# One column by transposes, fewer running-sum products, later operands 128 bytes further on, and one DVE order changed

## The chip, the cores and the metric

The kernel is one program on one core of a Trainium2 chip. The metric is the device time of one execution in microseconds (us); smaller is better. The engines are named as the profile names them: PE is TensorE's matmuls, PEld its loads of the stationary operand, DVE is VectorE, ACT is ScalarE, POOL is GpSimd, SP is the engine that issues most DMAs.

## The reference

The input is 256 tokens of width 1024, all in float32. A first block computes `h @ w_in` and splits it into four branches (a gated delta rule in chunks of 64, latent attention, spatial gating, forgetting attention), gates and sums them, and follows with `w_out` and a squared-ReLU feed-forward of width 4096. A second block has two layers: a state-space mixer with a short convolution, then sliding-window attention, each with a SwiGLU feed-forward of width 2816 and a gated embedding. What the change touches is four pieces of it:

```
# gated delta rule                              # chunks of 64 tokens
gc = jnp.cumsum(g, axis=-1)
decay = jnp.where(tril, jnp.exp(gc[..., :, None] - gc[..., None, :]), 0.0)
kb = k * beta[..., None]
# forgetting attention
cum = jnp.cumsum(log_f, axis=1)
s = s + (cum[..., :, None] - cum[..., None, :])
# state-space mixer                             # chunks of 128 tokens, 16 heads
a_cs = jnp.cumsum(da, axis=2)
decay_ls = jnp.exp(jnp.where(causal, a_cs[t] - a_cs[s], -jnp.inf))
y_diag = jnp.einsum('bclsgr,bcsgrp->bclgrp', cb[..., None] * decay_ls, xdt)
y = (y_diag + y_off + xs * d_skip) * jax.nn.silu(z)
```

Each of these decays needs a running sum over tokens twice: down the partitions (a column, one value for each token) and along a row that all partitions hold.

## The kernel before, in words

**Products.** Nearly all work is products of 256 tokens with weight matrices. Weights stream in units of 1024 columns: SP brings a unit into `raw`, ACT copies it to `whi` in the format fp32r (the high half), POOL subtracts and leaves the low half in `wlo`, and PE multiplies. Every product is made of three passes: high by high, high by low, low by high (function `product`, L1942 on; `unit_T`, L1910 on, is the same with one token tile at a time; `half`, L2145 on, is half a unit). In mode T the tokens' operand is stationary and 512 columns of `whi` or `wlo` move (L1960 to L1962, L1918 to L1920, L2167 to L2169); in modes F and B the weights are stationary and the tokens in `XT` move.

**Where the operands lie.** `raw`, `whi`, `wlo`, `X` and `XT` are allocated first; `whi`, `wlo` and `XT` start 128 bytes past a multiple of 256 in each partition. The split operands of the other stages (`BRhi`, `FFhi`, `PThi`, `BYhi`, `Hhi`, `AThi` and their low halves) are allocated later and start at a multiple of 1024 (`MQhi`, `MQlo`: 192 past a multiple of 256). All steps within these buffers are multiples of 512 bytes.

**Order of the work.** Each engine's order is written out by hand, with semaphores between the engines. PE's order interleaves the chained small work (the `mm` calls, all recorded as L1982, and transposes) with units of products, which fill PE's time while DVE and ACT work.

**Running sums and rows.** A running sum down the partitions is a small `mm` with a triangle of ones as stationary operand. A row was made by `mm` with the un-summed column, spread over 128 columns, as stationary operand and the triangle as moving one; for `beta`, with the identity.

**State-space heads.** There are eight groups of four heads (`hb` = 0 to 7). For a group, PE makes four rows (`rows`), DVE subtracts the column and masks (`decays`, L1627), ACT takes the exponential, DVE multiplies by the scores (`products`, L1636), and PE multiplies by the values (`heads_out`). After each second group DVE adds the other parts and gates the pair's output (`finished`, L1643 and L1647). `heads_out` of the next pair writes the same bank of PSUM and waits for that (`b_yd`); it also waits for its own `products` (`b_m`). PE's fill between the groups is half units of the products `sc0` and `sh0`.

Of the kernel before, what the change touches and what calls it, by code (L numbers as in the profile page):

```python
# [22 lines left out]
P = 128  # L23
# [202 lines left out]
def build(nc, a, out):  # L226
# [8 lines left out]
    with ctx:  # L235
# [55 lines left out]
        attn_sum = attn_sum2[:, 0]  # L291
        attn_inv2 = sb("attn_inv2", [P, 2, 4, 2])
        attn_inv = attn_inv2[:, 0]


        m1 = ExitStack()
# [782 lines left out]
        def _(v):  # L1079
# [551 lines left out]
            def products(hb):  # L1631
                v.wait_ge(S["b_e"], hb + 1)
                if hb >= 4:

                    v.wait_ge(S["b_y"], hb - 3)
                V.scalar_tensor_tensor(out=em[:, hb % 4], in0=pm[:, row_bank(hb), :].rearrange("p (r s) -> p r s", s=P),  # L1636
                                       scalar=1.0, in1=cbm[:, hb // 2, :].unsqueeze(1).to_broadcast([P, 4, P]),
                                       op0=ALU.min, op1=ALU.mult).then_inc(S["b_m"], 1)

            def finished(b):  # L1640
                y = yd[:, b // 2, (b % 2) * W:(b % 2 + 1) * W]
                v.wait_ge(S["b_y"], 2 * b + 2)
                link(V.tensor_tensor(pm[:, 2, :], pm[:, 2, :], y, ALU.add))  # L1643
                v.wait_ge(*evac_at("dt"))
                for c in range(2):
                    v.wait_ge(*evac_at(f"mz{c}"))
                V.tensor_tensor(y, pm[:, 2, :], zz[:, b // 2, (b % 2) * W:(b % 2 + 1) * W], ALU.mult)\  # L1647
                    .then_inc(S["b_yd"], 1)
            decays(0)
            decays(1)  # L1650
            for hb in range(8):
                products(hb)
                if hb < 6:
                    decays(hb + 2)
                if hb % 2:
                    finished(hb // 2)
            short_input(0)
            v.wait_ge(S["y_ss"], 1)
            link(variance(rv[:, 0:4], ss[:, 0:4], W, 1e-5))
# [207 lines left out]
        def _(pe):  # L1867
# [113 lines left out]
            def mm(o, lhs, rhs, start=True, stop=True, **k):  # L1981
                return T.matmul(o, lhs, rhs, start=start, stop=stop, **k)  # L1982

            def flat(i, n=P):

                return pm[:, i // BANK, i % BANK:i % BANK + n]


            def keep_busy(count):

# [38 lines left out]

            pe.wait_ge(S["dn_qkn"], 1)  # L2030
            pe.wait_ge(S["dn_g"], 1)
            for t in range(NT):
                mm(pm[:, 0, 4 * t:4 * t + 4], con("tri64"), dng[:, t, :])
                mm(pm[:, 0, 8 + 4 * t:12 + 4 * t], con("blk64"), dng[:, t, :])
            mm(pm[:, 0, 16:20], con("tri"), nlf[:, 0, :])
            mm(pm[:, 0, 20:24], ones, nlf[:, 0, :], stop=False)
            mm(pm[:, 0, 20:24], con("tri"), nlf[:, 1, :], start=False).then_inc(S["dn_gc"], 1)
            from_x("fq", 0, 2)
            pe.wait_ge(S["dn_gcs"], 1)

            for h in range(4):
                for t in range(NT):
                    i = (h * NT + t) * P
                    mm(flat(i), dng[:, t, h:h + 1].to_broadcast([P, P]), con("tri64"))
                    last = mm(flat(2 * BANK + i), beta[:, t, h:h + 1].to_broadcast([P, P]), ident)
            last.then_inc(S["dn_rows"], 1)
            from_x("fq", 2, 4)
            from_x("fk", 0, 1)
# [179 lines left out]
            pe.wait_ge(*turned("cqkv")(1))  # L2228
            for h in range(4):
                row = pm[:, 2 + h // 2, (h % 2) * TOK:(h % 2 + 1) * TOK]  # L2230
                mm(row, nlf[:, 0, h:h + 1].to_broadcast([P, P]), span("tri", "ones"), stop=False)
                last = mm(row[:, P:TOK], nlf[:, 1, h:h + 1].to_broadcast([P, P]), con("tri"), start=False)
            last.then_inc(S["f_rows"], 1)
            from_branch("br0_1")
            product("uq0", MQhi[:, 0:2], MQlo[:, 0:2])
# [111 lines left out]
            for g in range(2):  # L2347
                last = T.transpose(pm[:, 3, g * P:(g + 1) * P], xbcT[:, 8 + g, 0:P], ident)
            last.then_inc(S["s_bt"], 1)
            for c in range(2):  # L2350
                mm(pm[:, 3, 2 * P + c * SSD_H:2 * P + (c + 1) * SSD_H], con("tri"), da[:, c, :])
            mm(pm[:, 3, 2 * P + 2 * SSD_H:2 * P + 3 * SSD_H], ones, da[:, 0, :]).then_inc(S["s_ac"], 1)
            from_x("mz1", 1, 3)
            pe.wait_ge(S["s_btc"], 1)
# [10 lines left out]
            def rows(hb):  # L2365

                c, first = hb // 4, 8 * (hb // 2 % 2) + 4 * (hb % 2)
                if hb >= 3:
                    pe.wait_ge(S["b_m"], hb - 2)
                elif hb == 2:  # L2370
                    pe.wait_ge(S["s_yod"], 1)
                for r in range(4):
                    last = mm(pm[:, row_bank(hb), r * P:(r + 1) * P],
                              da[:, c, first + r:first + r + 1].to_broadcast([P, P]), con("tri"))
                last.then_inc(S["b_row"], 1)

            def heads_out(hb):

                b, half = hb // 2, hb % 2
                pe.wait_ge(S["b_m"], hb + 1)  # L2380
                if b and not half:
                    pe.wait_ge(S["b_yd"], b)
                for r in range(4):
                    at = (4 * half + r) * SSD_D
                    x = (b % 2) * W + at
                    last = mm(pm[:, 2, at:at + SSD_D], em[:, hb % 4, r, :], xdt[:, b // 2, x:x + SSD_D])
                last.then_inc(S["b_y"], 1)
            rows(0)
            rows(1)
            from_x("sc0", 0, 1)  # L2390
# [229 lines left out]
```

## Time and profile before

| | |
|---|---|
| time, median of 3 runs | 1267.34 us (1266.71 to 1269.21) |
| the profiled execution's own time | 1270.26 us |
| its span, first to last instruction | 1268.4 us |
| mean granted clock of TensorE | 0.997 |
| PE busy | 1258.0 us, 99% of the span, 7611 instructions |
| DVE, ACT, POOL busy | 39%, 51%, 74% |
| DMA | 218.33 MB, mean 172 GB/s |

A float32 matmul (`mm`) leaves two records of PE; an fp32r product or a transpose leaves one. A record's duration holds the way through the array and overlaps the next one, so that what a matmul costs is read as the distance from its start to the next start.

### The profile page before, as it was taken

What the parts mean: (1) busy time and instruction counts of PE and PEld (TensorE: products, weight loads), DVE (VectorE), ACT (ScalarE), POOL (GpSimd) and SP (SyncE); (2) the same over time, 40 slices, a digit from 0 to 9 for tenths busy, and PEclk for the clock granted to TensorE, in tenths of its full rate; (3) what the DMA queues carried; (4) which work ended last, traced back from release to release, by engine and by line L of the source; (5) the groups of instructions that cost most, each with busy time, mean ns of one, the idle gap of its engine ahead of it and who ended that gap; (6) DMA issues with size and microseconds to landing.
All of it is one profiled execution on the core that took longest, in us unless ns stands there. A gap on an engine that the chain in (4) does not pass through costs nothing.

```text
span 1268.4 us, 18665 instructions
## 1 busy us (share of the span) xinstructions
PE 1258.0 (99%) x7611; PEld 1081.4 (85%) x7611; DVE 490.5 (39%) x893; ACT 650.3 (51%) x873; POOL 942.5 (74%) x409
## 2 busy tenths in 40 slices
PE   9999999999999999999999999999999999999998
PEld 7988888888888888899999788888879868888886
DVE  5535344552224320037662153332042674333025
ACT  5573555755457653344544464444355655444433
POOL 6946357756969898875588688889867666888964
PEclk9999999999999999999999999999999999999999
DMA  8735235534646655553456566665548435655641
GB/s 285 211 116 165 70 100 164 183 101 139 224 142 208 194 202 194 190 166 112 150 167 199 196 227 190 192 199 184 198 125 277 152 119 161 185 183 183 202 163 67
DMA packets 147739, 218.33 MB, mean 172 GB/s; under 512 B 9368, under 2 KB 79559, under 8 KB 147655
## 3 DMA queue, kind: packets, MB, share of 16 engines
q1 hardware_dynamic: 143664, 209.73, 52.2%
q10 hardware_dynamic: 3990, 7.42, 1.8%
q8 instruction: 60, 0.98, 0.3%
q14 instruction: 25, 0.20, 0.0%
HBM read 216.07 MB, written 1.05 MB: 171 GB/s over the span
## 4 chain that ended last, share of the span: by engine, by line
PE 96%; DVE 2%; DMA 1%; ACT 0%; POOL 0%; issue 0%; POOLq 0%; ACTq 0%; DVEq 0%
PE acc L1966 18%; PE acc L1960 13%; PE acc L1961 12%; PE acc L1962 12%; PE acc L1967 9%; PE pm L1982 7%; PE acc L1973 4%; PE acc L1975 4%; PE acc L1976 4%; PE acc L1918 2%; PE acc L1920 1%; PE acc L1919 1%; PE acc L2167 1%; PE acc L2169 1%; PE acc L2168 1%; PE pm L1880 1%
## 5 line engine op out<-in xcount | busy, mean ns | idle before, releaser
L581 POOL TENSOR_TENSOR wlo<-raw,whi 128x1024 fp32r<-128x1024 f32 (+4 forms) x404 | 941.8, 2358 | 313.9 <-ACT whi L595 312.8
L595 ACT ACTIVATE whi<-raw 128x1024 fp32r<-128x1024 f32 (+4 forms) x404 | 404.6, 1033 | 225.3 <-PE acc L1962 143.0
L1966 PE MATMUL acc<-XT,whi 128*128 128x512 f32 x960 | 335.6, 395 | 0.0
L1967 PE MATMUL acc<-XT,wlo 128*128 128x256 f32 x960 | 268.1, 279 | 0.0
L1966 PEld LDWEIGHTS acc<-XT,whi 128*128 128x128 f32 x960 | 180.0, 188 | 42.2
L1967 PEld LDWEIGHTS acc<-XT,wlo 128*128 128x128 f32 x960 | 181.0, 189 | 0.0
L1973 PE MATMUL acc<-XT,whi 128*128 128x256 f32 x432 | 123.2, 285 | 0.0
L1960 PE MATMUL acc<-whi,XT 128*128 128x512 f32 (+4 forms) x320 | 123.0, 385 | 0.0
L1976 PE MATMUL acc<-XT,wlo 128*128 128x256 f32 x432 | 122.2, 283 | 0.0
L1975 PE MATMUL acc<-XT,whi 128*128 128x256 f32 x432 | 122.2, 283 | 0.0
L1961 PE MATMUL acc<-wlo,XT 128*128 128x512 f32 (+4 forms) x320 | 119.5, 373 | 0.0
L1962 PE MATMUL acc<-whi,XT 128*128 128x512 f32 (+4 forms) x320 | 119.5, 373 | 0.0
L1973 PEld LDWEIGHTS acc<-XT,whi 128*128 128x128 f32 x432 | 82.9, 192 | 0.6 <-issue 0.5
L1975 PEld LDWEIGHTS acc<-XT,whi 128*128 128x128 f32 x432 | 82.9, 192 | 0.1
L1976 PEld LDWEIGHTS acc<-XT,wlo 128*128 128x128 f32 x432 | 82.8, 192 | 0.0
L1960 PEld LDWEIGHTS acc<-whi,XT 128*128 128x128 f32 x320 | 60.1, 188 | 11.6 <-issue 1.5
L1962 PEld LDWEIGHTS acc<-whi,XT 128*128 128x128 f32 x320 | 60.2, 188 | 10.1
L1961 PEld LDWEIGHTS acc<-wlo,XT 128*128 128x128 f32 x320 | 60.2, 188 | 9.4 <-issue 0.5
L595 ACT ACTIVATE Hhi<-pm 128x512 fp32r<-128x512 f32 x22 | 13.2, 598 | 83.9 <-DVE pm L1769 83.9
L1961 PE MATMUL acc<-wlo,Hhi 128*128 128x512 f32 x136 | 53.7, 395 | 0.0
L1960 PE MATMUL acc<-whi,Hhi 128*128 128x512 f32 x136 | 53.7, 395 | 0.0
L1962 PE MATMUL acc<-whi,Hlo 128*128 128x512 f32 x136 | 53.6, 394 | 0.0
(413 smaller groups left out, 1986.2 us busy)
## 6 DMA issues: line engine op xcount, KB each, us to landing
raw<-in_w_in SPq DMA_DIRECT2D x68, 512.0 KB, 3.5
raw<-in_w_ff SPq DMA_DIRECT2D x64, 512.0 KB, 3.8
raw<-in_w_gate SPq DMA_DIRECT2D x44, 512.0 KB, 3.6
raw<-in_w_up SPq DMA_DIRECT2D x44, 512.0 KB, 3.6
raw<-in_w_down SPq DMA_DIRECT2D x44, 512.0 KB, 4.0
raw<-in_w_in_mix SPq DMA_DIRECT2D x36, 512.0 KB, 4.1
raw<-in_w_branch SPq DMA_DIRECT2D x16, 512.0 KB, 3.7
raw<-in_w_out_mix SPq DMA_DIRECT2D x16, 512.0 KB, 3.2
```

The source lines that it names most:

```text
L581: nc.gpsimd.tensor_tensor(piece(wlo, u), piece(raw, u), piece(whi, u).bitcast(F32), ALU.subtract).then_inc(S["w_lo"], 1)
L595: return nc.scalar.activation(out_, in_, func, **k)
L1918: T.matmul(o, hi[:, k, tok], wh, start=k == 0 and name not in CONTINUED, stop=False)
L1960: T.matmul(o, hi[:, k, tok], wh, start=opens, stop=False)
L1961: T.matmul(o, hi[:, k, tok], wl, start=False, stop=False)
L1962: last = T.matmul(o, lo[:, k, tok], wh, start=False, stop=done)
L1966: T.matmul(acc[:, n % 2, f, :], wh[:, fs], XT[:, :, k, :], start=opens, stop=False)
L1967: last = T.matmul(acc[:, n % 2, f, 0:TOK], wl[:, fs], XThi[:, k, :], start=False, stop=done)
L1973: T.matmul(o, wh[:, fs], hi[:, k, :], start=opens and f % 2 == 0, stop=False, skip_group_check=True)
L1975: T.matmul(o, wh[:, fs], lo[:, k, :], start=False, stop=False, skip_group_check=True)
L1976: last = T.matmul(o, wl[:, fs], hi[:, k, :], start=False, stop=done, skip_group_check=True)
L1982: return T.matmul(o, lhs, rhs, start=start, stop=stop, **k)
```

## The change

There are four edits. A buffer `apart` of 128 bytes, which nothing uses, is allocated before all later buffers, so that these start 128 bytes further on. The rows are made by PE transposes of a column: of the summed column (`gcs`, `ncs`, `acs`) that DVE has already written, or of `beta`, spread over 128 columns as before. Running sums of the same triangle are put into one `mm` each. On DVE `finished` of a pair is placed behind the `products` of the next group. Before the first rows of the state-space heads PE also waits for `s_acc`, the summed columns.

```diff
+        sb("apart", [P, 32])
...
             decays(0)
             decays(1)
-            for hb in range(8):
+            products(0)
+            decays(2)
+            for hb in range(1, 8):
                 products(hb)
+                if hb % 2 == 0:
+                    finished(hb // 2 - 1)
                 if hb < 6:
                     decays(hb + 2)
-                if hb % 2:
-                    finished(hb // 2)
+            finished(3)
...
+            def row_of(o, col):
+
+                return T.transpose(o, col.to_broadcast([P, P]), ident)
...
-            for t in range(NT):
-                mm(pm[:, 0, 4 * t:4 * t + 4], con("tri64"), dng[:, t, :])
-                mm(pm[:, 0, 8 + 4 * t:12 + 4 * t], con("blk64"), dng[:, t, :])
-            mm(pm[:, 0, 16:20], con("tri"), nlf[:, 0, :])
-            mm(pm[:, 0, 20:24], ones, nlf[:, 0, :], stop=False)
-            mm(pm[:, 0, 20:24], con("tri"), nlf[:, 1, :], start=False).then_inc(S["dn_gc"], 1)
+            both = [ap.rearrange("p t h -> p (t h)") for ap in (dng[:], nlf[:])]
+            mm(pm[:, 0, 0:8], con("tri64"), both[0])
+            mm(pm[:, 0, 8:16], con("blk64"), both[0])
+            mm(pm[:, 0, 16:24], con("tri"), both[1])
+            mm(pm[:, 0, 20:24], ones, nlf[:, 0, :], start=False, skip_group_check=True).then_inc(S["dn_gc"], 1)
...
-                    mm(flat(i), dng[:, t, h:h + 1].to_broadcast([P, P]), con("tri64"))
-                    last = mm(flat(2 * BANK + i), beta[:, t, h:h + 1].to_broadcast([P, P]), ident)
+                    row_of(flat(i), gcs[:, t, h:h + 1])
+                    last = row_of(flat(2 * BANK + i), beta[:, t, h:h + 1])
...
-                mm(row, nlf[:, 0, h:h + 1].to_broadcast([P, P]), span("tri", "ones"), stop=False)
-                last = mm(row[:, P:TOK], nlf[:, 1, h:h + 1].to_broadcast([P, P]), con("tri"), start=False)
+                for t in range(NT):
+                    last = row_of(row[:, t * P:(t + 1) * P], ncs[:, t, h:h + 1])
...
-            for c in range(2):
-                mm(pm[:, 3, 2 * P + c * SSD_H:2 * P + (c + 1) * SSD_H], con("tri"), da[:, c, :])
+            mm(pm[:, 3, 2 * P:2 * P + 2 * SSD_H], con("tri"), da[:].rearrange("p c h -> p (c h)"))
...
-                    last = mm(pm[:, row_bank(hb), r * P:(r + 1) * P],
-                              da[:, c, first + r:first + r + 1].to_broadcast([P, P]), con("tri"))
+                    last = row_of(pm[:, row_bank(hb), r * P:(r + 1) * P], acs[:, c, first + r:first + r + 1])
...
+            pe.wait_ge(S["s_acc"], 1)
             rows(0)
             rows(1)
```

How the instructions stand on DVE in the state-space heads before: `pm<-pm,acs,ct` is `decays` (x4, x8: four for each group), `em<-pm,cbm` is `products`, and the pair of `TENSOR_TENSOR` rows is `finished`.

```order
L1627 SCALAR_TENSOR_TENSOR pm<-pm,acs,ct 128x128 x8
L1636 SCALAR_TENSOR_TENSOR em<-pm,cbm 128x512
L1627 SCALAR_TENSOR_TENSOR pm<-pm,acs,ct 128x128 x4
L1636 SCALAR_TENSOR_TENSOR em<-pm,cbm 128x512
L1627 SCALAR_TENSOR_TENSOR pm<-pm,acs,ct 128x128 x4
L1643 TENSOR_TENSOR pm<-pm,yd 128x512
L1647 TENSOR_TENSOR yd<-pm,zz 128x512
L1636 SCALAR_TENSOR_TENSOR em<-pm,cbm 128x512
L1627 SCALAR_TENSOR_TENSOR pm<-pm,acs,ct 128x128 x4
```

And the same place of DVE now, one line number up:

```order
L1628 SCALAR_TENSOR_TENSOR pm<-pm,acs,ct 128x128 x8
L1637 SCALAR_TENSOR_TENSOR em<-pm,cbm 128x512
L1628 SCALAR_TENSOR_TENSOR pm<-pm,acs,ct 128x128 x4
L1637 SCALAR_TENSOR_TENSOR em<-pm,cbm 128x512
L1628 SCALAR_TENSOR_TENSOR pm<-pm,acs,ct 128x128 x4
L1637 SCALAR_TENSOR_TENSOR em<-pm,cbm 128x512
L1644 TENSOR_TENSOR pm<-pm,yd 128x512
L1648 TENSOR_TENSOR yd<-pm,zz 128x512
L1628 SCALAR_TENSOR_TENSOR pm<-pm,acs,ct 128x128 x4
```

The third `products` stands ahead of the first `finished` where it stood behind it, and so for each pair.

On PE, before, around the third group's rows (`pm<-ct,da`) and the first `heads_out` (`pm<-xdt,em`):

```order
L1975 MATMUL acc<-XT,whi 128x256
L1976 MATMUL acc<-XT,wlo 128x256
L1982 MATMUL pm<-ct,da 128x128 x4
L1982 MATMUL pm<-xdt,em 128x64 x4
L1982 MATMUL pm<-ct,da 128x128 x4
L2158 MATMUL acc<-XT,whi 128x256
```

And now (L1994 is the transpose in `row_of`):

```order
L1979 MATMUL acc<-XT,whi 128x256
L1980 MATMUL acc<-XT,wlo 128x256
L1994 MATMUL pm<-ct,acs 128x128 x4
L1986 MATMUL pm<-xdt,em 128x64 x4
L1994 MATMUL pm<-ct,acs 128x128 x4
L2164 MATMUL acc<-XT,whi 128x256
```

Nothing has changed its place on PE; the four matmuls of a group of rows are four transposes of `acs`. ACT, POOL and SP have the same rows in the same order before and now.

## Rows read from the trace of the kernel before

**Rows 1.** The page: the chain that ended last, share of the span by engine.

```profile
PE 96%; DVE 2%; DMA 1%; ACT 0%; POOL 0%; issue 0%; POOLq 0%; ACTq 0%; DVEq 0%
```

**Rows 2.** Waits of all engines: who waited for whom.

```profile
POOL wlo L581 <- ACT whi L595: 312.8, 159, 10.7
```

**Rows 3.** Timeline of PE, stationary operand `XT`: start us, duration us.

```profile
309.87 0.39 PE L1961 MATMUL acc<-wlo,XT 128*128 128x512 f32 x1
...
331.18 0.40 PE L1962 MATMUL acc<-whi,XT 128*128 128x512 f32 x1
```

**Rows 4.** Timeline of PE, stationary operand `FFhi` or `FFlo`.

```profile
484.92 0.39 PE L1961 MATMUL acc<-wlo,FFhi 128*128 128x512 f32 x1
...
508.38 0.40 PE L1960 MATMUL acc<-whi,FFhi 128*128 128x512 f32 x1
508.63 0.40 PE L1961 MATMUL acc<-wlo,FFhi 128*128 128x512 f32 x1
```

**Rows 5.** Groups by line and shape: count, busy us, mean ns, idle before.

```profile
L1961 PE MATMUL acc<-wlo,XT 128*128 128x512 f32 x240 | 93.6, 390 | 0.0
L1961 PE MATMUL acc<-wlo,Hhi 128*128 128x512 f32 x136 | 53.7, 395 | 0.0
```

**Rows 6.** Timeline of PE: the running sums of the first block.

```profile
75.19 0.95 PE L1982 MATMUL pm<-dng,ct 128*128 128x4 f32 x8
...
76.67 0.48 PE L1960 MATMUL acc<-whi,XT 128*128 128x512 f32 x1
```

**Rows 7.** Timeline of PE: the delta rule's rows, first one and what follows them.

```profile
82.21 0.38 PE L1982 MATMUL pm<-ct,dng 128*128 128x128 f32 x2
...
85.70 0.48 PE L1960 MATMUL acc<-whi,XT 128*128 128x512 f32 x1
```

**Rows 8.** Timeline of PE: the forgetting attention's rows.

```profile
206.59 2.78 PE L1982 MATMUL pm<-ct,nlf 128*128 128x256 f32 x16
209.13 0.47 PE L1960 MATMUL acc<-whi,BRhi 128*128 128x512 f32 x1
```

**Rows 9.** Timeline of PE: sixteen transposes.

```profile
252.98 1.91 PE L2260 MATMUL pm<-ct,fx 128*128 128x128 f32 x16
254.65 0.48 PE L1960 MATMUL acc<-whi,BRhi 128*128 128x512 f32 x1
```

**Rows 10.** Timeline of PE: state-space heads.

```profile
618.68 1.00 PE L1982 MATMUL pm<-xdt,em 128*128 128x64 f32 x8
619.52 1.11 PE L1982 MATMUL pm<-ct,da 128*128 128x128 f32 x8
620.39 0.36 PE L2158 MATMUL acc<-XT,whi 128*128 128x256 f32 x1
...
621.91 1.00 PE L1982 MATMUL pm<-xdt,em 128*128 128x64 f32 x8
...
625.12 1.00 PE L1982 MATMUL pm<-xdt,em 128*128 128x64 f32 x8
```

**Rows 11.** Timeline of DVE, same stretch.

```profile
617.81 0.68 DVE L1636 SCALAR_TENSOR_TENSOR em<-pm,cbm 128x512 f32<-128x512 f32 x1
...
622.94 0.70 DVE L1643 TENSOR_TENSOR pm<-pm,yd 128x512 f32<-128x512 f32 x1 [1.14 <-PE pm L1982]
623.68 0.69 DVE L1647 TENSOR_TENSOR yd<-pm,zz 128x512 f32<-128x512 f32 x1
```

**Rows 12.** Timeline of ACT, same stretch.

```profile
622.85 1.07 ACT L595 ACTIVATE pm<-pm 128x512 f32<-128x512 f32 x2
```

**Rows 13.** Timeline of PE: the longest wait.

```profile
1043.48 1.12 PE L1890 MATMUL pm<-ct,X 128*128 128x128 f32 x4 [2.61 <-DVE X L1695]
```

**Rows 14.** Stretches: length, busy (count) by engine, granted clock, DMA share, GB/s.

```profile
1046.00:1050.00 4.00, 4.00 (x11) 3.14 (x10) 3.75 (x10) 2.49 (x5) 1.18 (x1) 0.50 0.79 253
...
613.00:642.00 29.00, 29.00 (x251) 28.86 (x250) 20.17 (x49) 14.82 (x22) 12.87 (x7) 1.00 0.33 105
243.00:255.00 12.00, 12.00 (x79) 10.55 (x78) 1.78 (x2) 6.64 (x6) 8.73 (x4) 1.00 0.60 189
```

## The prediction

> **What bounds the kernel.** I read the chain of waits first. 96% of the span is PE's own work [rows 1], so a us less of PE's work is a us less of time wherever PE doesn't then wait for another engine. The waits say how much room the others have: POOL waits 312.8 us in all for ACT's high halves [rows 2] while its share of the span is 74%, and ACT is at 51%, so the weights keep up with a PE that is 1% faster. PE's one long wait is 2.61 us at 1043 us, on DVE's layer norm [rows 13]; no edit shortens it. So I price each edit on PE, from start to start in its timeline, and then look at the one place where DVE and ACT are nearly as late as PE: the state-space heads [rows 10 to 12].
>
> **Price of a transpose.** A row of 128 columns is now a float32 matmul of two records. The delta rule has 16 of them between 82.21 and 85.70 us: 3.49 / 16 = 0.218 us each [rows 7]. Sixteen transposes take 252.98 to 254.65: 1.67 / 16 = 0.104 us each [rows 9]. I read starts, since the mean durations of the two kinds are about equal and would show no gain. The trace has no transpose of a column spread over 128 columns. Its bounds are these two prices, 0.104 and 0.218 us. I take the lower, because spreading costs an ordinary matmul nothing: the `heads_out` matmuls, whose stationary operand isn't spread, take 618.68 to 619.52, 0.84 / 4 = 0.21 us each [rows 10], as much as the spread ones.
>
> **Delta rule.** The rows save 16 x (0.218 - 0.104) = 1.8 us. What waits for them on DVE and ACT starts from their end, and PE's fill behind them is unchanged, so nothing is late that wasn't. The running sums are seven small matmuls in 75.19 to 76.67, 1.48 us or 0.21 each [rows 6]; four remain. A matmul of eight columns instead of four is still bound by its weights at this size, so three go: 0.6 us.
>
> **Forgetting attention.** Eight matmuls take 206.59 to 209.13, 2.54 us [rows 8]; eight transposes take 8 x 0.104 = 0.8. Saved: 1.7 us. No engine is near waiting for these rows, since DVE works on the gating until then. The state-space running sum loses one small matmul: 0.2 us.
>
> **State-space heads.** 32 matmuls become transposes. In full this would be 32 x 0.114 = 3.6 us, but here little of it arrives. I follow PE with the old times. Three groups of rows stand ahead of the first `heads_out`, so PE is ready for it 3 x 0.45 = 1.3 us before 618.68. DVE's first `products` runs 617.81 to 618.49 [rows 11], and what stands ahead of it on DVE is the gating of the state's output, which starts when it did. `heads_out` starts at 618.6: 0.1 us gained, 1.2 us of a wait. Then 0.84 of `heads_out`, 0.42 of rows, and 1.52 of fill (620.39 to 621.91), the same again, and PE is ready for the third `heads_out` at 624.2, 0.9 before the old 625.12 [rows 10].
>
> There the moved instruction decides. Before, `finished` ran when the second `heads_out` was done, at 622.94, and the third `products` behind it. Now `products` goes first, and it needs the exponential that ACT makes at 622.85, behind a table load and the gate's activation; two take 1.07 us, so the first is there at 623.4 [rows 12]. ACT doesn't get there sooner, since its work from the first exponential on is unbroken. `products` ends at 624.1 (0.68 us), `finished` at 625.5 (0.70 + 0.69 and the gap between them), and PE starts the third `heads_out` at 625.6, 0.5 us later than before and 1.4 us after it was ready. Behind `products` stand `finished` and the fifth group's `decays` on DVE; who waits for them is PE alone. In the later pairs the exponential is early, so from 625.6 on the groups of rows still to come pass their gain on: three behind that point, 3 x 0.45 = 1.3. In sum the stage gives 1.3 - 0.5 = 0.8 us. In the old DVE order `finished` would be done at 623.9 and the third `heads_out` would start at about 624.6; so the new order costs 0.7 to 1 us here. Bounds of the stage: from 0.5 us lost (nothing passes behind the wait) to 3.6 gained. I take 0.8. The added wait for `s_acc` costs nothing: DVE writes these sums before PE's last two units of `mz1`, which stand ahead of the rows in PE's order.
>
> **The 128 bytes.** Two stretches of the same three-pass product differ only in where the stationary operand lies. With `XT`, 94 matmuls take 309.87 to 331.18: 21.31 / 94 = 226.7 ns each [rows 3]. With `FFhi` and `FFlo`, 102 take 484.92 to 508.63: 23.71 / 102 = 232.5 ns [rows 4]. The grouped view says it for all: mean duration 390 ns with `XT`, 395 with `Hhi` [rows 5]. `XT` has the same offset modulo 256 bytes as the moving `whi` and `wlo` (128), the others have 0; after the change all have 128. The matmuls with such an operand are, by the code, (16 + 32 + 16 + 44 + 8 + 4) k tiles of branches, f2, mo, fd, ao and pw x 2 column halves x 2 token tiles x 3 passes = 1440. If the offset is the cause, each gets 5 ns (the grouped means; 5.8 by the two stretches): 1440 x 5 = 7.2 us. The trace can't tell offset from place, since `XT` is also the only one of these operands allocated early. Bounds: 0, and 1440 x 5.8 = 8.4; the other side is rival B. I take the 7.2: the two stretches share everything but this operand, moving slots and banks of PSUM included.
>
> **Sum.** 1.8 + 0.6 + 1.7 + 0.2 + 0.8 + 7.2 = 12.3 us. Against the profiled execution: 1270.26 - 12.3 = 1258.0, with a span of 1256.1. That execution stands 2.9 above the median, which makes 1267.34 - 12.3 = 1255.0; I say 1255.2.
>
> **Rivals.**
> A, the offset does nothing. For it: the pace could hang on the place, and no row excludes this. Against it: `FFhi` and `Hhi` begin 28 KB apart and share the slower pace [rows 4, 5], as they share the offset. The time: only 5.1 us go, 1262.2. The Trainium skill, TensorE: Matmul & The Clock Gate, Step-by-step: what each phase is for, says that moving and stationary operands have read ports of their own, so that loading the next weights takes no bandwidth from the running matmul. By that rule addresses play no part and A holds; the 226.7 against 232.5 ns speak against it, or want another cause.
>
> B, slower: equal offsets make the two reads meet. The place is the same 1440 matmuls. Slow steps exist in the trace: 508.38 to 508.63 is 0.25 us between two starts [rows 4]. If the pace became 241 ns, 1440 x 8.6 = 12.4 us would be added and 5.1 saved: 1274.6. It decides from a pace of 236 ns on (1440 x 3.5 = 5.1). Against it: `XT` has this very offset and is the fast one.
>
> C, the spread column as a transpose is as dear as the matmul. Then rows give nothing: 0.8 us of running sums, 7.2, and in the heads a loss of 0.5 by the order: 1267.3 - 7.5 = 1259.8. Nothing but the missing row speaks for it.
>
> D, the new waits slow the clock. Behind the 2.61 us wait [rows 13] the granted clock is 0.50 from 1046 to 1050 [rows 14], level 1.2 GHz in place of 2.4. The two waits that I expect in the heads, 1.2 and 1.4 us, are shorter and 7 us apart, and now that stretch has 1.00. If it fell for as long, 4 to 6 us at half pace would cost 2 to 3 us: 1258. The Trainium skill, same page, Part 4: PE-mode transpose, says that transposes don't count as busy for the clock. By that rule the 56 new ones would add to the risk; 48 transposes between 243 and 255 us leave the clock at 1.00 [rows 14], so I raise D by a few hundredths only.
>
> **Chances.** The forecast (all terms, 1252.5 to 1258) 0.56; A 0.28; B 0.04; C 0.04; D 0.05; the rest, 0.03, is something unseen. A range from 1252.5 to 1263.3 holds the forecast, A with 1 us around it, C and D. What a measurement of this kernel can tell from no change is 0.2%, 2.5 us: faster means below 1264.8. Forecast, A, C and D all are; allowing for errors of sizes in A, faster 0.89, within 0.2% 0.06, slower 0.05 (B).
>
> **What would show it.** The `row_of` records start 0.104 to 0.11 us apart, one for each row. PE's 1440 matmuls run at 227 to 228 ns from start to start, mean duration 390; at 232 A is right, above 236 B. In the heads PE waits twice, before the first `heads_out` (1.2 us, for `products`) and before the third (1.4, for `finished`), and the third `products` on DVE starts right after ACT's exponential, ahead of the first `finished`. The stretch from the first rows to the last `heads_out` is only 0.8 us shorter. The forecast is wrong if PE's busy matmuls don't change their pace, or if PE waits anywhere else for DVE or ACT.

## The result, and the profile after

Runs of the two kernels taken by turns on one chip:

| | median | range | runs |
|---|---|---|---|
| before | 1269.19 us | 1266.71 to 1270.38 | 7 |
| after | 1263.77 us | 1258.29 to 1264.14 | 7 |

The ratio is 0.995 (95% interval 0.9938 to 0.9962): faster by 5.4 us of the medians, where 12.3 were forecast. The time lies 8.6 us above the forecast 1255.2 and above its range; 1.9 of the 8.6 are the kernel before itself, whose median is now 1269.19 and not the 1267.34 that the forecast started from. The profiled execution of after took 1263.77 us, its span 1261.9, 6.5 less than the span before.

The chain of waits of after, by engine; it answers to [rows 1]:

```profile
PE 91%; DVE 4%; ACT 2%; DMA 1%; issue 1%; POOL 1%; ACTq 0%; POOLq 0%; DVEq 0%
```

PE still carries it, but DVE and ACT have risen from 2% to 6% together: there are waits that weren't there. The waits of PE in after name most of them (line waited for: us in total, times, longest):

```profile
PE pm L1894 <- DVE X L1699: 3.9, 4, 2.7
PE acc L1964 <- DVE merged L1386: 1.5, 1, 1.5
PE pm L1986 <- DVE yd L1648: 1.4, 1, 1.4
...
PE pm L1986 <- DVE em L1637: 1.1, 1, 1.1
```

The first is the layer norm's wait of [rows 13]. `yd` and `em` are the two waits in the state-space heads that the prediction gave 1.4 and 1.2 us. `merged` is new and wasn't forecast. Two smaller ones are new as well, from PE's timeline in after:

```profile
603.81 1.96 PE L1986 MATMUL pm<-xe,bmt 128*128 128x512 f32 x4 [0.27 <-DVE xe L1584]
...
984.76 0.88 PE L2475 MATMUL pm<-ct,wS 128*128 128x128 f32 x6 [0.48 <-DVE wS L1841]
```

The own operands' matmuls (stationary `FFhi`, `Hhi` and so on) by start, in after; they answer to [rows 4]:

```profile
483.27 0.39 PE L1965 MATMUL acc<-wlo,FFhi 128*128 128x512 f32 x1
...
506.39 0.39 PE L1965 MATMUL acc<-wlo,FFhi 128*128 128x512 f32 x1
```

102 matmuls in 23.12 us are 226.7 ns each, the pace that only `XT` had [rows 3]. The grouped means of after answer to [rows 5] and bring a third row into play, the 960 products in which `XT` moves and `whi` is stationary (L1966 before, L1970 now):

```profile
L1970 PE MATMUL acc<-XT,whi 128*128 128x512 f32 x960 | 339.6, 399 | 0.0
L1965 PE MATMUL acc<-wlo,XT 128*128 128x512 f32 x240 | 93.6, 390 | 0.0
L1965 PE MATMUL acc<-wlo,Hhi 128*128 128x512 f32 x136 | 52.9, 389 | 0.0
```

In the trace of before, which the prediction didn't read there, the same group is:

```profile
L1966 PE MATMUL acc<-XT,whi 128*128 128x512 f32 x960 | 335.6, 395 | 0.0
```

`Hhi` went from 395 to 389 ns as forecast and `XT` as stationary operand stayed at 390, while the 960 went from 395 to 399. That is a loss inside busy time: no view of waits can show it.

Where the span's 6.5 us came from, start to start on PE in the two traces:

| part | forecast | profile pair |
|---|---|---|
| own operands' pace | -7.2 | -7.6 |
| delta rule's rows | -1.8 | -1.8 |
| running sums, block 1 and state space | -0.8 | -0.8 on PE, +0.2 as a wait for `xe` |
| forgetting rows | -1.7 | -1.7 on PE, +1.7 as a wait |
| heads | -0.8 | -0.9 |
| `XT` products with `XT` moving | not priced | +4.0 |
| a wait for the embedding's `wS` at 984 us | not priced | +0.7 |
| sum | -12.3 | -6.2 (span: -6.5) |

**The forgetting rows.** PE in after, behind the spatial gating's sums; it answers to [rows 8]:

```profile
203.99 1.04 PE L1994 MATMUL pm<-ct,ncs 128*128 128x128 f32 x8
204.79 0.48 PE L1964 MATMUL acc<-whi,BRhi 128*128 128x512 f32 x1
...
212.05 0.45 PE L1964 MATMUL acc<-whi,MQhi 128*128 128x384 f32 x1 [1.54 <-DVE merged L1386]
```

and DVE in the same stretch:

```profile
204.19 1.67 DVE L1393 SCALAR_TENSOR_TENSOR pm<-pm,colA,s_b 128x256 f32<-128x256 f32 x4 [6.16 <-PE pm L1986]
205.90 1.23 DVE L1398 TENSOR_TENSOR pm<-pm,sgu 128x1024 f32<-128x1024 f32 x1
207.04 0.34 DVE L1402 SCALAR_TENSOR_TENSOR fD<-pm,ncs,ct 128x128 f32<-128x128 f32 x1
...
209.65 1.22 DVE L1408 TENSOR_TENSOR BRlo<-pm,BRhi 128x1024 fp32r<-128x1024 f32 x1
210.78 2.35 DVE L1386 TENSOR_TENSOR merged<-acc,gt 128x1024 f32<-128x1024 f32 x2
```

The rows take 0.80 us (203.99 to 204.79), as forecast. But DVE's chain starts when PE's `swT` sums end, just ahead of the rows: gating, eight `fD` decays, `BRlo`, and only then `merge(0, 0)` (L1386), which empties the accumulator that the first `MQhi` product needs. The chain is as long as before. PE's stretch between the sums and that product is now 1.7 us shorter and starts to wait: the step onto `MQhi` is 1.93 us instead of 0.23.

**The moving `XT` products.** In these stages (f1 of block 1 with 256 pairs, the SwiGLU products of both layers with 352 each) a 512-column matmul with `whi` and a 256-column one with `wlo` alternate. In after:

```profile
779.80 0.40 PE L1970 MATMUL acc<-XT,whi 128*128 128x512 f32 x1
...
790.40 0.40 PE L1970 MATMUL acc<-XT,whi 128*128 128x512 f32 x1
```

30 pairs in 10.60 us are 353.3 ns a pair. In another execution of the same kernel (`e7_after_again` below), at the same place:

```profile
779.57 0.39 PE L1970 MATMUL acc<-XT,whi 128*128 128x512 f32 x1
...
789.97 0.39 PE L1970 MATMUL acc<-XT,whi 128*128 128x512 f32 x1
```

10.40 us for 30, 346.7 ns. From start to start there are two repeating patterns: 230, 117 ns over and over (in some stretches 231, 112, 233, 117, which is as long for a pair), or 241, 120, 236, 113, 233, 117. A stretch takes one of them in its first few matmuls and keeps it to its end. In f1 this happens behind a short break: its first eight pairs run in the slow sequence in every profile of this order, and the pattern is taken anew behind the small matmuls that follow them. The slow one (S) costs 1.7 us in f1 and 2.4 in each layer's stage over the fast one (F). Before's profile has F, F, S for the three stretches, after's S, S, S: 1.7 + 2.4 = 4.1 us, the table's 4.0. The means of the group of 960 tell it without any timeline: 392 ns where all three stretches are fast, 395 with one layer slow, 399 with all slow.

### The profile page after: what moved, and what is told of

Read it like the earlier page. It is cut to its first block, busy times and chain, and to the rows that moved or that the text cites. A ratio compares the mean times of both kernels' runs of the same rounds, so it can differ in the third digit from the quotient of the medians.

```text
span 1261.9 us, 18537 instructions
## 1 busy us (share of the span) xinstructions
PE 1246.5 (99%) x7547; PEld 1072.8 (85%) x7547; DVE 490.8 (39%) x893; ACT 650.1 (52%) x873; POOL 941.6 (75%) x409
## 4 chain that ended last, share of the span: by engine, by line
PE 91%; DVE 4%; ACT 2%; DMA 1%; issue 1%; POOL 1%; ACTq 0%; POOLq 0%; DVEq 0%
PE acc L1970 18%; PE acc L1964 12%; PE acc L1965 12%; PE acc L1966 12%; PE acc L1971 9%; PE pm L1986 6%; PE acc L1977 4%; PE acc L1979 4%; PE acc L1980 4%; PE acc L1922 2%; PE acc L1923 1%; PE acc L1924 1%; PE acc L2173 1%; PE acc L1999 1%; PE acc L2175 1%; PE acc L2174 1%
## 5 line engine op out<-in xcount | busy, mean ns | idle before, releaser
L1970 PE MATMUL acc<-XT,whi 128*128 128x512 f32 x960 | 339.6, 399 | 0.0
L1970 PEld LDWEIGHTS acc<-XT,whi 128*128 128x128 f32 x960 | 180.4, 188 | 44.9
L1966 PE MATMUL acc<-whi,XT 128*128 128x512 f32 (+4 forms) x320 | 119.4, 373 | 0.0
L1966 PEld LDWEIGHTS acc<-whi,XT 128*128 128x128 f32 x320 | 60.1, 188 | 10.0
L1966 PE MATMUL acc<-whi,Hlo 128*128 128x512 f32 x136 | 52.9, 389 | 0.0
```

The source lines that it names most:

```text
L1966: last = T.matmul(o, lo[:, k, tok], wh, start=False, stop=done)
L1970: T.matmul(acc[:, n % 2, f, :], wh[:, fs], XT[:, :, k, :], start=opens, stop=False)
```

## The experiments

All medians are in us, with their range; the ratios are to before on the same chip. F and S are the patterns of the three stretches in the profiled execution. The heads are the stretch from the first rows to the start of the matmul behind the last `heads_out`. The medians of before beside these runs were 1269.70 (e1 to e4), 1269.37 (e5 to e8), 1269.38 (e9 to e12) and 1269.15 (e13, e14).

| run | edit | median (range) | ratio, 95% interval | pattern | heads |
|---|---|---|---|---|---|
| e1 | before, `apart` 128 bytes | 1264.02 (1262.72 to 1266.65) | 0.9955, 0.9942 to 0.9968 | F S S | 28.55 |
| e2 | after, no `apart` | 1265.44 (1264.61 to 1266.80) | 0.9968, 0.9956 to 0.9980 | F F S | 27.60 |
| e3 | after, DVE's old order | 1259.45 (1258.24 to 1261.87) | 0.9923, 0.9911 to 0.9935 | S S F | 27.01 |
| e4 | before, `apart` 256 bytes | 1269.80 (1266.65 to 1274.32) | 1.0000, 0.9990 to 1.0011 | F F S | 28.54 |
| e5 | e3, merge early | 1261.19 (1256.09 to 1263.49) | 0.9933, 0.9916 to 0.9950 | F S S | 27.00 |
| e6 | after, merge and rows early | 1256.06 (1255.06 to 1257.58) | 0.9895, 0.9880 to 0.9911 | S S F | other start |
| e7 | after again, one execution | 1258.82 | | S F F | 27.61 |
| e8 | before again, one execution | 1267.08 | | F F F | 28.53 |
| e9 | e6, merge earlier still | 1255.80 (1255.08 to 1258.36) | 0.9890, 0.9876 to 0.9904 | F S F | other start |
| e10 | e9, grouped pairs | 1254.14 (1253.53 to 1254.44) | 0.9873, 0.9860 to 0.9885 | steady | other start |
| e11 | after, unwaited entry | 1262.92 (1259.52 to 1264.12) | 0.9938, 0.9922 to 0.9955 | S S F | |
| e12 | after, old forgetting rows | 1262.61 (1259.67 to 1263.95) | 0.9936, 0.9921 to 0.9950 | S S S | |
| e13 | before, grouped pairs | 1268.71 (1268.34 to 1269.50) | 1.0001, 0.9992 to 1.0011 | steady | 28.54 |
| e14 | after, grouped pairs | 1258.71 (1258.35 to 1260.22) | 0.9924, 0.9910 to 0.9939 | steady | 27.61 |

**e1 and e2: the 128 bytes alone, and all the rest alone.** e1 is before with one line more, e2 is after without it:

```
+        sb("apart", [P, 32])
```

> The kernel before with the 128 bytes alone. Theory P (offset sets the pace): the 1440 matmuls with FF, H, BY, BR, AT, PT operands run at 227 ns from start to start, 7.5 to 8 us less. Theory L (the shift also drives the products with XT moving in two pieces, L1966 and L1967, into their slow repeating pattern of 353.4 ns a pair instead of 346.7): all three stretches with such products (f1, the first and the second fg/fu) are at 353.4, and the net is 8 minus 4 = 4 us faster than the profiled before. Rival C (that pattern falls by chance, whatever the layout): the three stretches show a mixture of 346.7 and 353.4, and single executions of one kernel differ in steps of 1.7 and 2.4 us (256 and 352 pairs x 6.7 ns).

> The changed kernel without the 128 bytes: transposes, joined sums and the new DVE order alone. Theory P: the 1440 matmuls are back at 232.4 ns. PE saves 1.8 + 0.6 + 0.2 us, 0.9 in the heads, and the forgetting rows' 1.7 are eaten by a wait of 1.7 before uq0, so 3.3 to 3.5 us faster than before at the same pattern of the XT products. Theory L: the XT products are at 346.7 ns a pair in f1 and the first fg/fu as in the profile of before. Rival C: a mixture that differs from before's.

In e1 the own operands' matmuls run at 227.1 ns instead of 232.4, all other steps as before; the time falls by about 5.7 us, not 7.6, with two slow stretches in its profile. In e2 they run at 232.4, and it is 4.3 us below before by the medians and 3.5 by the two profiled executions, which both have F F S (3.3 to 3.5 were expected), with the `merged` wait and the heads as in after. So the pace belongs to the shift and nothing else, and the `merged` wait doesn't.

**e4: the same line with 256 bytes.** It moves every later buffer too, but leaves the offset modulo 256.

```
+        sb("apart", [P, 64])
```

> The kernel before with 256 bytes in place of 128: the later operands move, but their offset modulo 256 is as before. Theory P (the offset against whi and wlo): pace stays at 232.4 ns, time as before. Rival A (place, not offset, or the new neighbours): pace changes, to 227 if any move does it.

The own pace stays at 232.6 and the time at 1269.8. The grouped rows, first e1 (128 bytes), then e4 (256); with `XT` the mean is 390 ns in both:

```profile
L1967 PE MATMUL acc<-XT,whi 128*128 128x512 f32 x960 | 338.0, 397 | 0.0
L1962 PE MATMUL acc<-wlo,Hhi 128*128 128x512 f32 x136 | 52.9, 389 | 0.0
```

```profile
L1962 PE MATMUL acc<-wlo,Hhi 128*128 128x512 f32 x136 | 53.7, 395 | 0.0
```

It is the offset modulo 256 bytes that counts, not the place: what the trace of before couldn't tell is told. The moving `whi` and `wlo` stay 128 past a multiple of 256 in every run, so it isn't shown whether the distance between the two operands sets the pace or the stationary one's own offset. The Trainium skill, TensorE: Matmul & The Clock Gate, Step-by-step: what each phase is for, has it that loading weights takes no read bandwidth from the running matmul. Read as rival A read it, as a rule in which addresses play no part, it doesn't fit the 232.4 against 227.2 ns; the measurement decides.

**e3: DVE's old order in the heads.**

```
-            products(0)
-            decays(2)
-            for hb in range(1, 8):
+            for hb in range(8):
...
-                if hb % 2 == 0:
-                    finished(hb // 2 - 1)
...
-            finished(3)
+                if hb % 2:
+                    finished(hb // 2)
```

> The changed kernel with the DVE order of before in the heads. Theory O (the new order costs here): PE's wait before the third heads_out falls from 1.57 to about 0.4 us, the first stays at 1.2, a third small one of 0.3 may come before the fifth, and the stage from the first rows to the last heads_out is 0.7 us shorter than the changed kernel's 27.6. Rival N (the order is neutral or helps): the stage is as long or longer.

The heads take 27.01 us against 27.61. DVE in e3, around the third `products`:

```profile
618.79 0.70 DVE L1644 TENSOR_TENSOR pm<-pm,yd 128x512 f32<-128x512 f32 x1 [1.15 <-PE pm L1983]
619.52 0.69 DVE L1648 TENSOR_TENSOR yd<-pm,zz 128x512 f32<-128x512 f32 x1
620.13 0.68 DVE L1637 SCALAR_TENSOR_TENSOR em<-pm,cbm 128x512 f32<-128x512 f32 x1
```

against the same in after:

```profile
619.53 0.69 DVE L1637 SCALAR_TENSOR_TENSOR em<-pm,cbm 128x512 f32<-128x512 f32 x1 [2.20 <-ACT pm L596]
620.14 0.69 DVE L1644 TENSOR_TENSOR pm<-pm,yd 128x512 f32<-128x512 f32 x1
```

In the new order DVE waits 2.20 us for ACT's exponential with `finished` behind it; in the old one `finished` fills that time. The new order costs 0.6 us; the prediction said 0.7 to 1. The median fell by 4 us, far more than this 0.6. That is what first pointed at something that no edit had touched, and e3's profile has a fast third stretch.

**e5, e6 and e9: taking the waits away.** e5 is e3 with `merge(0, 0)` ahead of the `fD` decays:

```
     (spatial gating)
+            merge(0, 0)
     (decays of the forgetting attention, BRlo)
-            merge(0, 0)
```

> The changed kernel with the old DVE order in the heads (as the run before it with that order) and DVE's first gating product, merge(0, 0), ahead of the forgetting attention's decays instead of behind them. Theory M (the forgetting rows were the cover of DVE's chain to merge(0, 0), which frees the accumulator for uq0): PE's wait of 1.7 us before the first MQ matmul goes, and the time is 1.5 to 1.7 us below that run at the same patterns of the XT products. Rival (the wait has another end, such as the weights of uq0): it stays.

DVE in e5:

```profile
206.31 1.23 DVE L1398 TENSOR_TENSOR pm<-pm,sgu 128x1024 f32<-128x1024 f32 x1
207.45 1.21 DVE L1386 TENSOR_TENSOR merged<-acc,gt 128x1024 f32<-128x1024 f32 x1
208.58 0.34 DVE L1403 SCALAR_TENSOR_TENSOR fD<-pm,ncs,ct 128x128 f32<-128x128 f32 x1
```

and PE, at the starts of the two products with this operand (`uq0`, `uq1`):

```profile
210.75 0.34 PE L1961 MATMUL acc<-whi,MQhi 128*128 128x384 f32 x1
...
213.58 0.45 PE L1961 MATMUL acc<-whi,MQhi 128*128 128x384 f32 x1 [0.58 <-DVE merged L1386]
```

The first `MQhi` product no longer waits (a step of 0.23 us in place of 1.93): `merge(0, 0)` was what PE waited for. But `merge(0, 1)`, which stands behind the decays and `BRlo` as before, is now late for the second one, onto which the step is 0.92 us. So 1.7 us go and 0.7 come back 2.8 us later. (What was expected of e9 takes these 0.92 us for a rest of the first wait.) The median didn't follow (1261.19, with a range of 7.4 us): the profile has two slow stretches. A gain of 1 us can't be read from medians that scatter so; it is read in the trace.

e6 has the new DVE order and the early merge, and in the heads two groups ahead of the wait for the state: `rows(0)` and `rows(1)` on PE before the state-output product, their decays on DVE before its gating:

```
+            pe.wait_ge(S["s_acc"], 1)
+            rows(0)
+            rows(1)
             pe.wait_ge(S["s_stc"], 1)
     (state-output product)
...
     (DVE: decays(0), decays(1), and then)
+            v.wait_ge(S["s_yo"], 1)
+            V.tensor_tensor(by_head(off), by_head(off), per_head(eac[:, 0, :]), ALU.mult)
```

> The changed kernel (new DVE order kept) with merge(0, 0) ahead as in the run beside it, and in the heads rows(0), rows(1) and their decays ahead of the state's output product and its gating. Theory H (PE's two waits of 1.2 and 1.6 us come from DVE's gating standing ahead of the first decays, and from ACT's second exponential pair behind a table load): both waits fall below 0.3 us, the stage from the first product of the state's output to the last heads_out is 2.3 to 2.7 us shorter, and the new order is the better one here. Rival: the waits only move, to the state's output product or to heads_out of the second pair.

Both waits of the heads are gone. From the first of rows and state-output product to the matmul behind the last `heads_out` it is 26.5 us in e6 against 29.3 in after, 2.8 less; 2.3 to 2.7 were expected. The first three `heads_out` in e9, which shares this part, come without one; from the second to the third it is 2.71 us, against 4.27 in after (617.43 to 621.70):

```profile
610.09 1.10 PE L1986 MATMUL pm<-xdt,em 128*128 128x64 f32 x8
...
612.89 1.00 PE L1986 MATMUL pm<-xdt,em 128*128 128x64 f32 x8
...
615.60 1.00 PE L1986 MATMUL pm<-xdt,em 128*128 128x64 f32 x8
```

e9 is e6 with `merge(0, 0)` still earlier, ahead of DVE's wait for the spatial sums, where it was idle 4 us and more:

> The kernel of e6 (rows early, new DVE order) with merge(0, 0) still earlier on DVE: ahead of the spatial gating's sums. Theory M: the rest of PE's wait before the first MQ matmul (0.92 us from start to start in e6, where an unwaited step is 0.23) goes, so 0.7 us less than e6 at the same patterns of the XT products. Rival: DVE's later start on the gating makes BRlo of branch 2 or the decays late, and PE waits there instead.

```profile
202.56 1.22 DVE L1386 TENSOR_TENSOR merged<-acc,gt 128x1024 f32<-128x1024 f32 x1 [4.41 <-PE acc L1966]
204.35 1.67 DVE L1394 SCALAR_TENSOR_TENSOR pm<-pm,colA,s_b 128x256 f32<-128x256 f32 x4 [0.56 <-PE pm L1986]
```

The merge costs nothing there, `merge(0, 1)` is done earlier too, and PE waits before neither of the two `MQhi` products. The medians of e6 and e9 are equal within their scatter.

**e7 and e8: the same two kernels once more.**

> The changed kernel once more. Theory C (the pattern of the XT products is latched when each of the three stretches is entered, by chance of a few ns): at least one of the three stretches may be at 346.8 ns a pair instead of 353.5, and span and stretches agree: 1.7 us for f1, 2.4 for each fg/fu stretch. Theory L (the shift fixes it): all three at 353.5 again.

> The kernel before once more. Theory C: the three stretches may differ from 347, 347, 353.5 ns a pair. Theory L: they are the same again.

These two executions settle what the 4.0 us are. Nothing was edited, and after came at 1258.82 with S F F, 4.9 us below its first profile with S S S (2 x 2.4 = 4.8); before at 1267.08 with F F F, 3.2 below its first with F F S (2.4 of them by the pattern, the rest in the stretch from 1043 to 1053 us, where the first had the lower clock). The group of 960 in e7 and in e8:

```profile
L1970 PE MATMUL acc<-XT,whi 128*128 128x512 f32 x960 | 334.9, 393 | 0.0
```

```profile
L1966 PE MATMUL acc<-XT,whi 128*128 128x512 f32 x960 | 333.3, 392 | 0.0
```

**e10: a steady order of the pairs.** e9 with both 512-column matmuls of a k tile ahead of both 256-column ones:

```
 for f in range(width // P):
     fs = slice(f * P, (f + 1) * P)
     T.matmul(acc[:, n % 2, f, :], wh[:, fs], XT[:, :, k, :], start=opens, stop=False)
+for f in range(width // P):
+    fs = slice(f * P, (f + 1) * P)
     last = T.matmul(acc[:, n % 2, f, 0:TOK], wl[:, fs], XThi[:, k, :], ...)
```

> The kernel of e9 with the order inside the products of f1 and fg/fu changed: for each k tile both high-weight matmuls of 512 columns, then both low-weight ones of 256, instead of one of each in turn. Theory G (the slow pattern of 353.5 ns a pair belongs to the alternation of 512 and 256 columns): all three stretches lie at or below 347 ns a pair in every execution, single times scatter by under 1 us instead of up to 6, and the median is 3 to 5 us below e9's. Rival (alternation has no part in it): the stretches again fall on 347 or 353.5, or on something slower.

All three stretches run at 348.3 ns for a pair's two matmuls, and the single times lie within 0.9 us. The pace is steady, but it isn't the fast one: 347 ns or less was expected, and a median 3 to 5 us below e9's, where it is 1.7 below. It is the fastest version of the study: 1254.14, ratio 0.9873, about 9.6 us below after by the medians.

**e11: does the entry decide?** In the shifted layouts PE enters the first layer's stage with a short wait, and in seven of eight such profiles the slow pattern follows (not in e7). e11 lengthens the transposes ahead of it so that there is no wait:

```
-                turn_half(a_turn, 2 * i, 1, 1)
+                for f in (0, 1, 2, 3, 3, 3):
+                    (transpose of quarter f)
```

> The changed kernel with two more transposes (the last one repeated) just ahead of each fg/fu stretch, 0.2 us of work that fills PE's short wait there. Theory E (how PE enters a stretch latches its pattern for the whole stretch): the first step into the first fg/fu stretch is unwaited (27 instead of 133 to 151 ns to the next start) and that stretch changes from 353.5 to 347 ns a pair, 2.4 us less. Rival: the pattern is drawn whatever PE does at the entry; no change of the odds.

The entry had no wait (a step of 28 ns where after has 143) and the stretch was slow all the same. This is one profile, but the second layer's stage says the same: of ten profiles that enter it without a wait six are slow and four fast. The theory of the entry wait falls.

**e12: the forgetting rows as before, the rest as after.**

```
-                for t in range(NT):
-                    last = row_of(row[:, t * P:(t + 1) * P], ncs[:, t, h:h + 1])
+                mm(row, nlf[:, 0, h:h + 1].to_broadcast([P, P]), span("tri", "ones"), stop=False)
+                last = mm(row[:, P:TOK], nlf[:, 1, h:h + 1].to_broadcast([P, P]), con("tri"), start=False)
```

> The changed kernel with the forgetting attention's rows made by matmuls as before. Theory M: PE's wait before the first MQ matmul goes and the rows take 1.7 us more: the same time as the changed kernel within its own steps. Rival (the wait comes from something else that the change moved, such as the faster BR products): the wait stays at least in part and the kernel is up to 1.7 us slower.

PE in e12:

```profile
204.08 2.78 PE L1986 MATMUL pm<-ct,nlf 128*128 128x256 f32 x16
206.62 0.48 PE L1964 MATMUL acc<-whi,BRhi 128*128 128x512 f32 x1
...
212.17 0.39 PE L1964 MATMUL acc<-whi,MQhi 128*128 128x384 f32 x1
```

2.54 us of rows and no wait. `MQhi` starts 0.12 us later than in after, which has 0.80 us of rows and the wait. With S S S in both profiles the spans are 1261.6 and 1261.9. As the order stands, the 1.7 us saved here are worth nothing.

**e13 and e14: both kernels with the grouped order.** The edit of e10 alone, on before and on after. With no chance of a pattern on either side their difference is what the edits are worth.

> The kernel before with one edit: in the stages that multiply by XT's tiles in two pieces, both 512-column products with the weights' high part stand together, and then both 256-column ones with its low part, instead of by turns. Nothing is left out. Theory P (the whole shortfall of the change beyond the forgetting rows is the two repeating patterns): the three stretches run steadily at 348.3 ns per pair as in the run with this order on the change's side, single times scatter by 1.5 us or less, and the time is 1269.3 plus 960 pairs x (348.3 - about 347.5), 1269.5 to 1271. Rival Q (the shift costs somewhere else too): the same time for this kernel; what tells them apart is its distance from the changed kernel with the same edit.

> The changed kernel with the same one edit as the kernel before it: the two 512-column products together, then the two 256-column ones. Nothing is left out. Theory P: 348.3 ns per pair in all three stretches, and the distance to the kernel before with the same edit is the sum of the terms that held, 7.6 (own operands) + 1.8 + 0.6 + 0.2 + 0.9 = 11.1, less 0.7 to 1.0 of small new waits: 10.1 to 10.4 us, so 1259 to 1261. Rival Q: the distance stays at 5.4 to 6.5 us as in the first comparison, and the time is 1263 to 1265 though all stretches are steady; then 4 us are lost at a place that is not in these stretches.

The group of 960 has a busy time of 301.7 us and a mean of 396 ns in both. In e14 the pace is steady, two pairs from one of these rows to the next:

```profile
779.47 0.63 PE L1970 MATMUL acc<-XT,whi 128*128 128x512 f32 x2
...
792.71 0.63 PE L1970 MATMUL acc<-XT,whi 128*128 128x512 f32 x2
```

(13.24 us for 38 pairs, 348.4 ns.) The medians are 1268.71 and 1258.71: 10.0 us, where 10.1 to 10.4 were expected. The terms that held make 7.6 + 1.8 + 0.6 + 0.9 = 10.9; the state space's 0.2 came back as the wait for `xe` here too. Against them stands, in the two profiles, the clock behind the layer norm's wait: from 1036 to 1042 us e13 is granted 1.00 and e14 0.54, and the matmuls with the attention's operand there take 1.1 us longer. That leaves 9.8, which is the distance of the two profiled executions. That the medians differ by the same cause isn't shown. e13:

```profile
1036.00:1042.00 6.00, 6.00 (x26) 4.53 (x25) 4.01 (x7) 2.34 (x2) 5.67 (x3) 1.00 0.60 172
```

e14, with the same columns as [rows 14]:

```profile
1036.00:1042.00 6.00, 5.66 (x18) 4.38 (x17) 5.68 (x13) 2.50 (x5) 3.17 (x2) 0.54 0.53 160
```

The clock there isn't a matter of the kernel: the kernel before had 0.50 in its first profile [rows 14] and in e8, after the same wait (2.62 us for 2.61), has 1.00, and the two differ by 1.0 us there:

```profile
1046.00:1050.00 4.00, 3.33 (x18) 2.47 (x17) 3.75 (x10) 2.47 (x6) 1.38 (x1) 1.00 0.77 209
```

e13's twelve times lie within 1.2 us and e14's six within 1.9, where the 17 of before beside them span 6.0 (1266.84 to 1272.79). The same order also says what e9's moves are worth: e10 is 4.6 us below e14 by the medians, and the traces have 1.7 of them before `MQhi` and 2.8 in the heads.

## Why the prediction was wrong

The likeliest case held in its mechanism on PE and in nearly all its terms, and 6.9 us of the gain were missed: 1.7 by a step that failed, about 1 by smaller waits and the clock, and 4.6 by something that wasn't priced; about 0.5 came in above the forecast, mostly in the own operands' pace.

- **A transpose instead of a matmul: right.** The delta rule's 16 rows in after:

```profile
81.59 0.27 PE L1994 MATMUL pm<-ct,gcs 128*128 128x128 f32 x1
...
83.25 0.47 PE L1964 MATMUL acc<-whi,XT 128*128 128x512 f32 x1
```

  1.66 us against 3.49 [rows 7], 0.104 us each: the lower bound, as taken. A spread column costs a transpose nothing either; rival C is out. The heads' groups of four go at 0.09 us each. The running sums gave 0.6 and 0.2 on PE as forecast, but the 0.2 didn't arrive: PE came that much earlier to the product with `xe` and waited 0.27 us for it, as in every run with this edit and in none without.

- **"No engine is near waiting for these rows": the step that failed.** It looked at who waits for the rows themselves, and DVE doesn't. But the rows also stood on PE between the `swT` sums, which start DVE's chain, and the `MQhi` product, which waits for the end of that chain through its accumulator. In the trace of before `merge` ended at 213.37 + 1.22 = 214.59, and PE came to `MQhi` at 214.81, DVE's row first:

```profile
213.37 1.22 DVE L1385 TENSOR_TENSOR merged<-acc,gt 128x1024 f32<-128x1024 f32 x1
```

```profile
214.81 0.34 PE L1960 MATMUL acc<-whi,MQhi 128*128 128x384 f32 x1
```

  There were 0.2 us of slack, and the 1.7 us of rows were the cover. e12 shows that the saving is worth nothing as the order is, e5 and e9 that the wait is for `merge`, and goes when `merge` moves. The 0.2 us of the state-space sum failed by the same step.

- **Heads: right.** 0.93 us gained against 0.8. The two waits are there, 1.07 and 1.40 us for 1.2 and 1.4, the third `products` stands where it was put, behind ACT's exponential, and the new order costs 0.6 (e3) for 0.7 to 1.

```profile
614.61 1.10 PE L1986 MATMUL pm<-xdt,em 128*128 128x64 f32 x8 [1.07 <-DVE em L1637]
...
621.70 1.08 PE L1986 MATMUL pm<-xdt,em 128*128 128x64 f32 x8 [1.40 <-DVE yd L1648]
```

- **The 128 bytes: right in cause and size, incomplete in reach.** 232.4 to 227.2 ns from start to start, 7.6 us in the profile pair for the forecast 7.2 (1440 x 5.2 = 7.5); rival A, which named the place or nothing at all, is out by e1 and e4, though the time landed 1.6 us from its 1262.2 by other causes. Rival B is out too.

- **Not priced: the pairs with moving `XT`, the larger part of the miss.** The prediction read the other products' pace in two stretches and took these 960 pairs as fixed, a term put at nothing without a reason. Their two lines are 26% of the chain of before, and their two patterns stood in its trace (346.9 and 353.6 ns over the stages of the two layers, which run the same product). The shares can be read off e13 and e14. The edits are worth 10.0 us; between the medians of before and after stand 5.4; so 4.6 went with the patterns. Before loses 0.4 against its grouped version, after 5.1. (These medians come from different chips, on which those of before lie within 0.6 us.)

- **Rival D: out.** The stretch from 613 to 642 us keeps a granted clock of 1.00 with both waits in it:

```profile
613.00:642.00 29.00, 26.52 (x228) 26.11 (x227) 17.79 (x44) 18.84 (x30) 13.07 (x6) 1.00 0.35 110
```

**What stays open.** Why the shifted layout draws the slow pattern more often. In the first layer's stage the profiles of ungrouped kernels without the 128-byte shift were fast 4 times of 4 (before, e2, e4, e8), those with it slow 8 times of 9 (all but e7). In f1 it is 4 of 4 fast without and 6 of 9 slow with the shift; in the second layer's stage 3 of 4 are slow without it and 4 of 9 with it, so there the shift draws nothing. `XT`, `whi` and `wlo` themselves are where they were. A wait at the entry isn't it. The count is of single profiled executions, so the odds are rough, and it isn't shown that the shift and not something that comes with it sets them.

## What to carry to other kernels

Before time saved on the busiest engine is booked, find what other engine's chain runs beside the saved work, from the same start to the next meeting point: the smaller of saving and slack is what arrives. Read the start-to-start pace of every large group in several stages, not only of the groups that an edit touches; if one and the same product shows two paces, its time is a matter of chance that can swallow or fake an edit of a few us, and an order with one steady pace (348.3 ns a pair here) makes small edits measurable. Where stationary and moving operands can be placed freely, try them at equal offsets modulo 256 bytes: here it was 2.2% of the time of those matmuls.

## What the runs showed of the hardware

- An fp32r matmul of 512 columns whose moving operand starts 128 past a multiple of 256 bytes takes 232.4 ns from start to start with a stationary operand at a multiple of 256, and 227.2 with one at 128 as well (before, e1, e4).
- Alternating 512- and 256-column matmuls with a new stationary operand each fall into one of two repeating patterns, 346.7 or 353.3 ns a pair, at the start of a stretch, and keep it for the 90 to 125 us of it; two executions of one kernel differ in it (e7, e8). Grouped by twos they show 348.3 ns only, in nine stretches of nine (e10, e13, e14).
- Behind the layer norm's wait of 2.6 to 2.7 us at about 1040 us the granted clock is a matter of the execution: 0.50 (the level 1.2 GHz) over 4 us in before [rows 14], 1.00 in e8, the same kernel. Thirteen of the sixteen profiles have some microseconds of the lower level there; e8, e10 and e13 have none.
- 24 transposes of a single column spread over 128 in the first block, and 32 in the heads, cost 0.09 to 0.10 us each from start to start, and the mean granted clock stayed at 0.999.
